# Expert weights asked for in pieces of 1 MB, two under way at a time

## The reference, cut to what matters

```python
order = jnp.argsort(flat_e)                      # (token, expert) pairs, grouped by expert
...
def expert_block(args):
    xblk, e = args                               # rows of one expert
    hg, hu = jnp.split(xblk @ w_exp_in[e], 2, axis=-1)
    return (jax.nn.silu(hg) * hu) @ w_exp_out[e]
...
y_assign = yb[dest].reshape(n_tok, TOP_K, -1)
return jnp.einsum('tk,tkd->td', gate, y_assign)  # weighted sum of a token's two results
```

## Time and profile before

| | us |
|---|---|
| median of 3 runs | 2376.46 (2372.93 to 2376.68) |
| profiled execution, its own time | 2368.03 |
| its span, first to last instruction | 2366.1 |
| TensorE busy in the span | 2129.5 |
| idle time of VectorE before L894 that a store `yb<-yst` ended | 193.2 |
| DMA queue q1 (SyncE), share of 16 engines' span | 31.2% |
| DMA queue q10 (ScalarE) | 2.8% |

### The profile page before, as it was taken

How to read it: one execution, slowest core, us unless ns; L and a number is a source line. 1 busy time by engine, 2 the same in 40 slices (tenths; PEclk the granted TensorE clock), 3 DMA queues, 4 the chain that set the end, 5 groups by cost and what they waited for, 6 DMA issues and landing times. The chain is left out here.

```text
span 2366.1 us, 51954 instructions
## 1 busy us (share of the span) xinstructions
PE 2129.5 (90%) x21092; PEld 1350.6 (57%) x21092; DVE 976.2 (41%) x1976; ACT 430.3 (18%) x894; POOL 262.3 (11%) x430
## 2 busy tenths in 40 slices
PE   5999999949999998999998999899899499899987
PEld 3666654426666665466555555666444376567653
DVE  1333233352222221649866667455433522222226
ACT  1233221110000001211114454333211000000011
POOL 0000000002222122102010000000000122122212
PEclk9999999969999999999999999999999699999999
DMA  6111214148768762821030000654131568755847
GB/s 220 37 37 34 91 40 184 54 170 339 294 261 330 265 260 91 301 79 36 22 116 7 7 6 1 255 201 184 73 151 65 223 242 320 294 205 188 348 161 293
DMA packets 148632, 383.53 MB, mean 162 GB/s; under 512 B 11592, under 2 KB 71128, under 8 KB 146472
## 3 DMA queue, kind: packets, MB, share of 16 engines
q1 hardware_dynamic: 110160, 276.62, 31.2%
q0 software_dynamic: 16480, 82.77, 9.5%
q10 hardware_dynamic: 21880, 22.55, 2.8%
HBM read 336.89 MB, written 45.00 MB: 161 GB/s over the span
## 5 line engine op out<-in xcount | busy, mean ns | idle before, releaser
L307 PE MATMUL PS<-xT,W 128*128 128x352 f32 x960 | 286.6, 461 | 28.4 <-ACTq L316 28.4
L502 PE MATMUL PS<-wo,yT 128*128 128x512 f32 x576 | 260.2, 601 | 0.6 <-issue 0.6
L307 PEld LDWEIGHTS PS<-xT,W 128*128 128x128 f32 x960 | 183.3, 191 | 130.5 <-ACTq L316 28.4
L823 PE MATMUL PS<-w,yst 128*32 128x256 f32 x3360 | 203.3, 380 | 31.9 <-DVE yst L894 27.0
L812 PE MATMUL PS<-xT,yst 128*32 128x256 f32 x3648 | 212.1, 384 | 13.9 <-DVE yst L879 12.1
L1049 PE MATMUL PS<-xT,W 128*128 128x352 f32 (+1 forms) x672 | 202.4, 464 | 1.2 <-ACT xT L994 1.2
L854 ACT ACTIVATE yst<-PS 128x128 f32<-128x128 f32 x150 | 41.7, 278 | 800.2 <-PE PS L812 528.7
L812 PEld LDWEIGHTS PS<-xT,yst 128*32 128x32 f32 x3648 | 143.2, 111 | 71.4 <-issue 19.8
L823 PEld LDWEIGHTS PS<-w,yst 128*32 128x32 f32 x3360 | 128.2, 110 | 91.0 <-issue 45.4
L812 PE MATMUL PS<-yT,yst 128*32 128x256 f32 x3072 | 175.8, 379 | 0.0
L879 DVE STREAM_TRANSPOSE yst<-yst 128x256 f32<-128x256 f32 x150 | 66.6, 444 | 263.6 <-PE PS L812 255.9
(11 more groups left out here) (370 smaller groups left out, 2384.8 us busy)
## 6 DMA issues: line engine op xcount, KB each, us to landing
xT<-in_w_exp_in SPq DMA_DIRECT2D x24, 2048.0 KB, 14.7
w<-in_w_exp_out SPq DMA_DIRECT2D x22, 2048.0 KB, 15.3
yT<-in_w_exp_in SPq DMA_DIRECT2D x20, 2048.0 KB, 13.0
wo<-in_w_exp_in SPq DMA_DIRECT2D x20, 2048.0 KB, 14.5
xrn<-in_w_exp_out SPq DMA_DIRECT2D x10, 2048.0 KB, 15.9
yb<-yst ACTq DMA_DIRECT2D x150, 128.0 KB
W<-in_w_in_even SPq DMA_DIRECT2D x20, 512.0 KB, 3.9
xm<-xrn SPq DMA_DIRECT2D x18, 512.0 KB, 2.9
```

Source lines behind the costliest of these rows:

```text
L307: ins = nc.tensor.matmul(PS[:, n % 5, 0:CW], W5[:, p, k, :], xT[:, k, c * CW:(c + 1) * CW], start=(k == 0), stop=(k == KD - 1))
L502: ins = nc.tensor.matmul(PS[:, mix_bank(t) + n, :], yT[:, (k + 4 * l) % KD, t * P:(t + 1) * P], wo[:, k, n * 512:(n + 1) * 512], start=(fi ...
L823: ins = nc.tensor.matmul(PS[q * GR:(q + 1) * GR, 1, 0:2 * P], ht[:, k, :], w2[s][:, k, q * 2 * P:(q + 1) * 2 * P], start=(k == 0), stop=(k ...
```

## The change

From the third expert of a layer on, the three requests of 2 MB become six of 1 MB: four for the first matrix, two for the second. Two new semaphores, `e_piece0` and `e_piece1`, count the pieces that have landed, even ones and odd ones. Before it asks for a piece, SyncE waits until the piece two earlier has landed, across experts and layers as well, so that two are under way at most. The conditions that a buffer is free stay as they were. TensorE waits for both counts where it waited for one semaphore of the buffer. Experts 0 and 1 of each layer are loaded as before.

```diff
@@ -766,16 +766,28 @@
             sp.dma_start(w2[s], w2d[:, e, :, :]).then_inc(sem(f"e_in_w2_{s}"), 16)
 
         def sp_experts(sp, l):
+            w1d = io["w_exp_in"].rearrange("(e k p) n -> p e k n", p=P, k=KD)
+            w2d = io["w_exp_out"].rearrange("(e k p) n -> p e k n", p=P, k=F_EXP // P)
+
+            def piece(n, w, src):
+                count = 42 * l + 3 * (e - 2) + n // 2
+                if count > 0:
+                    sp.wait_ge(sem(f"e_piece{n % 2}"), 16 * count)
+                k = n % 4 * 2
+                sp.dma_start(w[:, k:k + 2, :], src[:, l * EXPERTS + e, k:k + 2, :]).then_inc(sem(f"e_piece{n % 2}"), 16)
+
             sp.wait_ge(sem("r_plan"), l + 1)
             sp.wait_ge(sem(f"e{l}_xtb"), 2 + 2)
-            load_w1(sp, l * EXPERTS + 2, 2)
-            load_w2(sp, l * EXPERTS + 2, 2)
-            for e in range(3, EXPERTS):
-                first = first_of(sp, e - 2)
-                sp.wait_ge(sem(f"e{l}_up"), first + 1)
-                load_w1(sp, l * EXPERTS + e, e % 3)
-                sp.wait_ge(sem(f"e{l}_down"), first + 1)
-                load_w2(sp, l * EXPERTS + e, e % 3)
+            for e in range(2, EXPERTS):
+                first = first_of(sp, e - 2) if e > 2 else None
+                if e > 2:
+                    sp.wait_ge(sem(f"e{l}_up"), first + 1)
+                for n in range(4):
+                    piece(n, w1[e % 3], w1d)
+                if e > 2:
+                    sp.wait_ge(sem(f"e{l}_down"), first + 1)
+                for n in range(4, 6):
+                    piece(n, w2[e % 3], w2d)
             sp.wait_ge(sem(f"e{l}_down"), first_of(sp, EXPERTS - 1) + 1)
             for s in range(3):
                 sp.dma_start(xres[:, s, :], xm[l][rows(s), :]).then_inc(sem(f"n_in_x{s}"), 16)
@@ -826,15 +838,23 @@
 
             g0, following = 0, first_of(pe, 1)
             for e in range(EXPERTS):
-                s, turn = e % 3, e // 3
-                per = 5 if s else 6
-                pe.wait_ge(sem(f"e_in_w1_{s}"), 32 * per * l + turn * 32 + 32)
+                s = e % 3
+                pieces = 16 * (42 * l + 3 * (e - 2))
+                if e < 2:
+                    pe.wait_ge(sem(f"e_in_w1_{s}"), 32 * l + 32)
+                else:
+                    for n in range(2):
+                        pe.wait_ge(sem(f"e_piece{n}"), pieces + 32)
                 part(pe)
                 up(s, g0)
                 if e > 0:
                     following = first_of(pe, e + 1) if e + 1 < EXPERTS else total_of(pe)
                     down((s + 2) % 3, g0 - 1)
-                pe.wait_ge(sem(f"e_in_w2_{s}"), 16 * per * l + turn * 16 + 16)
+                if e < 2:
+                    pe.wait_ge(sem(f"e_in_w2_{s}"), 16 * l + 16)
+                else:
+                    for n in range(2):
+                        pe.wait_ge(sem(f"e_piece{n}"), pieces + 48)
                 part(pe)
                 n = nc.s_assert_within(following - g0, 2, MAX_GR, skip_runtime_bounds_check_because="every expert has two granules or more in the plan")
                 with pe.Fori(0, n - 1) as j:
```

## The result

The changed kernel takes 2357.36 us (median of 4 runs, 2352.95 to 2357.56); the kernel before, beside it on the same chip, 2375.69 (4 runs, 2372.93 to 2376.68). The ratio is 0.992, 95% interval 0.9903 to 0.9937: 18 us faster. The forecast was 2331, 45 us faster: right in sign, the time inside the range, less than half of the gain. What came is close to the rival "Stalls go only in part", 2361.

A forecast was written before the change was run, and what follows sets the result against it. Slow result stores beside the weight stream were taken to stall TensorE in both expert stages; -58.5 (stalls) + 6 (left over) + 6.5 (late weights) = -46 us from the median 2376.46, said as 2331 us, range 2316 to 2362.

The forecast's parts named there:

- Stalls go only in part: Rival, 12%: pieces take 8.1 us, 259 GB/s; layer 1's end waits 14 us, half the stalls stay; 15 gained, 2361.
- What bounds: Both expert stages lose 60.2 us against a 5.18 us granule floor, through slow result stores; 58.5 us to be had.
- the queue lies empty for 2.6 + 2.9 - 3.3 = 2.2 us of that: Weight queue after each 1 MB piece: empty for 2.2 us, letting stores land in 6.2 us, 8.8 at most.
- all 58.5 us go: Expert stages: every avoidable store stall vanishes, 58.5 us, less 6 us left for stores meeting a piece and a gather.
- the 2.6 us from a landing to the next byte: Weight queue: fixed part of a 512 KB load's 3.9 us, taken as the gap before the next piece's first byte.
- The 2.9 us taken ahead, from the gather: DMA engines take packets some 2.9 us ahead, since a gather lands in 5.7 us under load against 2.8 quiet.
- Weights land later: End of layer 1, expert 15: weights slow to 293 GB/s as stores gain, so TensorE waits 6.5 us.
- Issue and waits: SyncE's extra requests, some 0.46 us each, are hidden; TensorE's second semaphore costs at most 0.1 us at 56 places.
- -58.5 + 6 + 6.5 = -46: Whole kernel: store stalls gone, 6 us of them left over, 6.5 us wait for weights; 46 us gained.
- The turns go on: Rival, 12%: weight queue never runs empty, stores keep taking turns at 6.68 us per granule; no change, 2376 us.
- Weights become the bound: Rival, 8%: three round trips per expert decide from 9.1 us a piece; at 10 us, 76 us more, 2452.
- What would show it: Signs in the profile after, for copy's idle time, projection steps, store landings, TensorE's one wait and piece landings.

The follow-up runs named there:

- the kernel with two requests: Kernel before, each store of a result asked for as two requests of 64 partitions instead of one: 2547.95 us, ratio 1.0723.
- the kernel with four requests: Kernel before, each store of a result asked for as four requests of 32 partitions x 256 floats instead of one: 2313.28 us, ratio 0.9731.
- the changed kernel with the split store: Changed kernel (1 MB pieces, two under way) with each store of a result asked for as four requests: 2323.23 us, ratio 0.9777.
- three and four pieces: Changed kernel with three pieces of 1 MB under way: 2371.35 us; with four pieces of 512 KB under way: 2351.82 us.

## Why the prediction was right or wrong

**What bounds: right.** The stores' stalls are worth what I read off: with them gone by another way, the kernel before takes 2313 us, 63 less in the medians and 57.9 in the stages, against 58.5 read.

**The step that failed: "the queue lies empty for 2.6 + 2.9 - 3.3 = 2.2 us of that".** From this came stores of 6.2 us and "all 58.5 us go". What the packets say: stores pass at about 20 per us when taking turns and at 74 when the queue is empty. For 23.7 on average the queue lies empty (23.7 - 19.8) / (74 - 19.8) = 7% of the time; with the 13 per us between two bursts shown above, the same sum gives 18%. The next piece follows about every 7.8 / 2 = 3.9 us, so that is 0.3 to 0.7 us per piece (an estimate, since turns may be shorter, as above): an eighth to a third of what I had. 24.7 packets per us were needed.

The term that was off most is the 2.6 us from a landing to the next byte. I had taken it from a lone load as all that is not movement. The kernel with one transfer of 2 MB under way shows it by itself. One transfer lands at 2002.39 and the next is asked for at 2002.41; this is what moved from 2002.05 to 2003.44 (packets, MB, share of 16 engines):

```profile
q0 software_dynamic: 43, 0.13, 28.1%
q10 hardware_dynamic: 118, 0.12, 23.7%
```

No weights at all, and 85 store packets per us. The last packet of weights ended 0.35 us before the landing, and the first of the next transfer started 1.1 us behind it (medians of 84 transfers). With 1.1 for 2.6 the formula gives 0.7 us, and with 3.9 us for a piece instead of 3.3 as well, 0.1. The 2.9 us taken ahead, from the gather, no run tests alone. I took a difference of three numbers of about 3 us, each from another queue or stretch, as safe, and put the store at 6.2 us where 9.7 was the edge.

Behind it lies what I had not looked at: through how many engines a store goes. Here are the signals of one store and one piece of the kernel after, us from their issue, in the order in which the engines gave them:

```
2000.98 store  0.99 9.30 9.44 9.55 9.64
1998.92 piece  4.42 4.44 4.56 4.83 4.85 4.92 4.99 5.00 5.01 5.02 5.53 7.37 7.43 7.45 7.47 7.64
```

A store has four late signals and an early one; in the kernel with two requests each request has two and an early one, and in the kernel with four requests each has up to sixteen. The Trainium skill ("DMA: Bandwidth & Descriptors", "Why a DMA increments its semaphore by 16 and not by 1") says that a request of SyncE or ScalarE uses the largest number of engines, up to 16, that divides the outermost size of both sides, that only these post an increment and that the issuer writes the rest at once. The trace agrees, and 2548, 2376 and 2313 us for outermost sizes of 2, 4 and 32 show what it is worth here. So 32 packets of a store queue up at each of four engines, and a piece is mostly done at 5 us and then waits for the last few engines to 7.6. Stores and pieces were slow in part for one reason, and the changed kernel with the split store shows how far: there the 13th and 14th signal of layer 1's pieces come at 5.6 and 5.8 us in the median instead of 7.4 and 7.5, but the last at 7.05 instead of 7.8. What holds that last engine no run tells.

**Weights land later: right in place, near in size.** One wait, at expert 15 of layer 1, 8.17 us and 1.7 more for a slow up projection behind it, where 6.5 were forecast (3 to 12 as the sign). The rival's 8.1 us per piece and 259 GB/s are the better numbers: pieces asked for from 1985 to 2045 land in 7.8 us in the median (7.5 to 8.4), 2.1 million bytes per 7.8 us, 269 GB/s. Its 14 us were too many. That 6.5 came so near is partly luck: TensorE was ready at 2250.2, 55.9 us after expert 13 was asked for (2194.26) and not 53.3, because stalls stayed, and the weights let it start after 64.1 us and not 59.8.

**Issue and waits: right.** Nothing in the chain stands for SyncE's requests (0.37 us each) or for the second semaphore; the bound of 0.1 us a place for the latter came from no row.

**Sum.** Forecast -58.5 + 6 + 6.5 = -46. Measured in the stages -30.4 + 9.8 = -20.6. Of the 25 us missing, 22 are stores and 3 are weights.

**Rivals.** "Stalls go only in part" came true in both halves: half of the stalls stay, and the end of layer 1 waits. Its gain of 15 is near 18. "The turns go on" is what three and four pieces do: even stores of 12 us. "Weights become the bound" came with one transfer, or with pieces of 512 KB two at a time. I gave these 12%, 12% and 8% beside a forecast that hung on one difference; 68% for it was too sure.

**What would show it.** Copy's idle time under 60 us: wrong, 168.6. Steps of 5.18: wrong, 5.6. Stores under 9 us: wrong. One wait of 3 to 12 us: right. Pieces in 5 to 8 us: right for the median of 7.8, though single ones took up to 9.8.

## What to carry to other kernels

When a small store is slow beside a bulk load, look first at how many DMA engines it goes through: an outermost size of 4 put 128 KB through four, and asking for it as four plain requests of 32 partitions gave 63 us where holding back the load gave 18. Holding back a load freed the stores here mostly in the moments when its queue was empty, and each such moment is lost to the load. A gain that is a small difference of large, borrowed times deserves the range of its parts, not its middle.

## What the runs showed of the hardware that was not expected

A wait of 8.17 us was enough to halve the clock. The stretch around its end, in the profile after (us; busy times of TensorE, its weight loads, VectorE, ScalarE and GpSimd; then granted clock, DMA share, GB/s):

```profile
2254.97:2261.80 6.83, 3.41 (x33) 1.82 (x37) 0.00 (x0) 0.00 (x0) 0.00 (x0) 0.50 0.90 322
```

TensorE had stood idle from 2250.2 to 2258.4. For the 6.83 us of the row the clock was granted at 0.50, the lower of its two levels (1.2 GHz); the up projection took 5.32 us where others take 3.66. So this wait cost a fifth more than its length. In the changed kernel with the split store a wait of 5.15 us cost 2.2 us more, 5.82 instead of 3.66, again with the clock at 0.50. And a bulk load is as slow as its slowest engine: eleven of sixteen signals of the piece above had come by 5.53 us, and it landed at 7.64.
